# A decoder trunk on one core: squares of a norm summed by two additions of whole chunks instead of one strided reduction

## The chip, the cores and the metric

The kernel runs on one core of one Trainium2 chip. The core has five engines that run their own queues and wait for each other by semaphores: TensorE (PE; its weight loads are listed as PEld), VectorE (DVE), ScalarE (ACT), GpSimd (POOL) and SyncE (SP). The metric is the time of one execution on the device in microseconds (us), as the median of several runs.

## The reference, cut to what matters

Two layers of a decoder trunk are computed for 1040 prompt tokens (16 of them learned) and 32 sample tokens, with a model width of 1024. Each layer has a mixer and an MLP, and each of these four is preceded by an RMS norm over the 1024 features:

```
def rmsnorm(x, g):
    xf = x.astype(jnp.float32)
    y = xf * lax.rsqrt(jnp.mean(xf * xf, axis=-1, keepdims=True) + EPS)
    return (y * g.astype(jnp.float32)).astype(x.dtype)
...
for layer in range(DEPTH):
    h = rmsnorm(x, norm_mix[layer])
    ...
    x = x + sqrelu_mlp(rmsnorm(x, norm_mlp[layer]), w_up[layer], w_down[layer])
```

What is left out is the mixer, a projection with convolution and attention in layer 0 and a pooling mixer in layer 1. The change lies in the sum of squares inside the mean of this norm.

## The kernel before

The residual stream `xT` stays in SBUF as 128 partitions x 8 chunks x 1072 tokens: a token's 1024 features lie in 128 partitions of 8 chunks. The tokens are worked on in three pieces of 368, 352 and 352 columns. All large products are done in fp32 by three matmuls each: activations and weights are split into a high and a low part (`act_hi`, `act_lo`, `w_hi`, `w_lo`), and `product` (L525 to L527) sums three of the four cross products. PE works through units of output, each in one of four PSUM banks; before a unit it waits until the bank's old content has been taken away (`out_freed`), which DVE mostly does.

A norm n (0 to 3) of piece p goes through these steps:

- ACT writes `act_hi` (the residual times the gain, L1052) and DVE `act_lo` (L1394).
- ACT squares four chunks (half 0, then half 1) into `norm_buf` (L1028, `norm_square`). There is one buffer, so the square of half 1 waits until half 0 has been summed (`norm_summed`).
- DVE sums the four chunks of the buffer into one row of columns of `norm_sum` (L1371, `norm_reduce`). This is the place of the change. It runs 24 times: 4 norms x 3 pieces x 2 halves.
- PE adds over the partitions with a matmul against a constant matrix (L581, `norm_stats`; L576 for norm 2), ACT takes the root (L1043), DVE the reciprocal (L1386, `norm_rsqrt`).

The order on each engine is written out by hand, program by program, and is the same before and after apart from the sums. In the first stage (norm 0, about the first 120 us) the steps of a norm are interleaved with the first 18 units of the input projection. ACT copies token tiles from PSUM to the residual (L1075, after PE has transposed them, L605). For a unit that holds queries or keys DVE multiplies by the norm's reciprocal root in PSUM (L1455), ACT squares it (L1124), PE averages it per head (L591), ACT takes the root (L1109), and `head_finish` on DVE takes the reciprocal (L1427) and writes the scaled product, `k_flat` or `qT` (L1433), which frees the bank. So in DVE's queue the two sums of a piece stand ahead of the L1455, L1427 and L1433 that free a bank for PE.

In the pooling stage (about 1210 to 1285 us) DVE scales products of PE into `z` (L1734) and adds windowed means to the residual (L1747, `add_windows`); the sums of norm 3 stand between those.

Two lines tie ACT and PE to the sums, the first in `norm_square`, before it overwrites the buffer, the second in `norm_stats`, which needs both halves:

```
act.wait_ge(norm_summed, i)
...
pe.wait_ge(norm_summed, 2 * k + 2)
```

Of the kernel before, what the change touches and what calls it, by code (L numbers as in the profile page):

```python
# [1 line left out]

# [7 lines left out]
ALU = mybir.AluOpType  # L33
ACT = mybir.ActivationFunctionType
AX_X = mybir.AxisListType.X
# [118 lines left out]
def trunk_kernel(nc, ins, outs):  # L154
# [5 lines left out]
    with ctx:  # L160
        def sem(name):
            return ctx.enter_context(nc.semaphore(name))
# [128 lines left out]

        norm_sq, norm_summed, norm_mean = sem("norm_sq"), sem("norm_summed"), sem("norm_mean")
        norm_root, norm_rs_done = sem("norm_root"), sem("norm_rs_done")
        norm_hi = sem("norm_hi")
        act_ready = sem("act_ready")
        head_scaled = sem("head_scaled")
        head_sq_done, head_mean = sem("head_sq_done"), sem("head_mean")
# [24 lines left out]
        def norm_pieces(n):  # L322
            return PIECES if n < 3 else PIECES1

        def norm_tensors(n):
            return (norm_buf0, norm_sum0) if n == 0 else (norm_buf, norm_sum)
# [1020 lines left out]
        def _(dve):  # L1347
# [16 lines left out]
            def norm_reduce(n, p, half_):  # L1364
                i = 2 * (3 * n + p) + half_
                c0, c1 = norm_pieces(n)[p]
                buf, total = norm_tensors(n)
                dve.wait_ge(norm_sq, i + 1)
                if i >= 2:
                    dve.wait_ge(norm_mean, i // 2)  # L1370
                nc.vector.tensor_reduce(total[:, half_, 0:c1 - c0], buf[:, :, 0:c1 - c0].rearrange("p c n -> p n c"),  # L1371
                                        AX_X, ALU.add).then_inc(norm_summed, 1)

            def norm_rsqrt(n, p):
                k = 3 * n + p
# [23 lines left out]
            def norm_splits(n, p):  # L1399
                for pair in range(4):  # L1400
                    norm_split_lo(n, p, pair)
                for half_ in range(2):
                    norm_reduce(n, p, half_)
# [6 lines left out]
            for pair in range(4):  # L1410
                norm_split_lo(0, 0, pair)
            norm_reduce(0, 0, 0)
            split_lo(1)
            norm_reduce(0, 0, 1)
            norm_rsqrt(0, 0)
            split_lo(2)
# [29 lines left out]
            for m in range(18):  # L1446
                grp, p, part = m // 9, (m % 9) // 3, m % 3
                c0, c1 = PIECES[p]
                n = c1 - c0
# [374 lines left out]
```

## Time and profile before

| | us |
|---|---|
| median of 3 runs (2044.83 to 2045.99) | 2045.95 |
| span of the profiled execution | 2043.0 |
| median less that span | 2.95 |
| PE busy | 2004.9 (98%) |
| DVE busy | 967.2 (47%) |
| ACT busy | 539.9 (26%) |
| POOL busy | 45.5 (2%) |

The span runs from the first to the last instruction of one profiled execution; the execution's own time beside it is not listed, and the median of the runs lies 2.95 us above the span. Busy times are sums over an engine's instructions. Times inside the profile count from the span's start.

### The profile page before, as it was taken

The page shows a single profiled execution, that of the slowest core. Times are in us where ns is not written, and L with a number is a line of the kernel's source. Part 1 is how long each engine was busy: PE and PEld are TensorE (multiplying, and loading weights), DVE is VectorE, ACT ScalarE, POOL GpSimd, SP SyncE. Part 2 cuts the span into 40 slices and gives each one's busy share as a digit, 9 for nine tenths or more (in the row PEclk, how much of TensorE's full clock was granted, in tenths as well). Part 3 has the DMA queues.
Part 4 walks back from the last instruction along what each step waited for, and adds up shares of the span by engine and source line. Part 5 has one row for each costly group of instructions (what it writes and reads, how often), then busy time and mean ns, then how long its engine had stood idle before and what let it go on. Part 6 is the DMA issues. An engine that isn't in the chain of part 4 may idle for free.

```text
span 2043.0 us, 30495 instructions
## 1 busy us (share of the span) xinstructions
PE 2004.9 (98%) x12458; PEld 1959.0 (96%) x12458; DVE 967.2 (47%) x1604; ACT 539.9 (26%) x965; POOL 45.5 (2%) x88
## 2 busy tenths in 40 slices
PE   6999999999999999999999999999999999999999
PEld 5888888999999999999999999999999999999998
DVE  5777776484333333333333487633333333333433
ACT  5333333143122121213121333313121221212131
POOL 1210000100000000000000000000000000000000
PEclk8899999999999999999999998999999999999999
DMA  5411101312111120211211110111211111211112
GB/s 204 146 47 32 32 32 58 99 42 61 42 42 41 41 62 21 62 41 41 62 41 42 42 42 5 31 53 41 62 41 41 41 41 41 62 31 51 52 32 85
DMA packets 132336, 106.42 MB, mean 52 GB/s; under 512 B 4771, under 2 KB 126919, under 8 KB 132240
## 3 DMA queue, kind: packets, MB, share of 16 engines
q1 hardware_dynamic: 126800, 90.52, 14.7%
q0 software_dynamic: 5216, 14.78, 2.3%
q8 instruction: 53, 0.87, 0.2%
q14 instruction: 19, 0.16, 0.0%
q10 hardware_dynamic: 248, 0.09, 0.0%
HBM read 94.64 MB, written 10.49 MB: 51 GB/s over the span
## 4 chain that ended last, share of the span: by engine, by line
PE 91%; DVE 6%; ACT 2%; issue 1%; DMA 0%; SPq 0%; DVEq 0%; ACTq 0%
PE out L525 29%; PE out L527 28%; PE out L526 28%; PE out L950 2%; PE turned L744 1%; DVE norm_sum L1371 1%; DVE head_sq L1427 1%; PE turned L727 1%; DVE act_lo L1394 1%; PE scores L693 1%; PE turned L581 0%; DVE w_lo L1361 0%; DMA raw<-in_w_in_even 0%; DVE rs L1386 0%; ACT act_hi L1052 0%
## 5 line engine op out<-in xcount | busy, mean ns | idle before, releaser
L525 PE MATMUL out<-act_hi,w_hi 128*128 128x352 f32 (+1 forms) x2160 | 714.9, 331 | 6.5 <-DVE qT L1433 2.8
L527 PE MATMUL out<-act_hi,w_lo 128*128 128x352 f32 (+1 forms) x2160 | 703.1, 326 | 0.0
L526 PE MATMUL out<-act_lo,w_hi 128*128 128x352 f32 (+1 forms) x2160 | 700.9, 325 | 0.0
L525 PE MATMUL out<-hid_hi,w_hi 128*128 128x352 f32 (+1 forms) x1536 | 501.3, 326 | 0.0
L527 PE MATMUL out<-hid_hi,w_lo 128*128 128x352 f32 (+1 forms) x1536 | 499.6, 325 | 0.0
L526 PE MATMUL out<-hid_lo,w_hi 128*128 128x352 f32 (+1 forms) x1536 | 497.7, 324 | 0.0
L525 PEld LDWEIGHTS out<-act_hi,w_hi 128*128 128x128 f32 x2160 | 408.3, 189 | 19.3 <-issue 12.3
L526 PEld LDWEIGHTS out<-act_lo,w_hi 128*128 128x128 f32 x2160 | 409.0, 189 | 1.4 <-issue 0.2
L527 PEld LDWEIGHTS out<-act_hi,w_lo 128*128 128x128 f32 x2160 | 408.2, 189 | 0.0
L1636 DVE TENSOR_TENSOR residual<-out,residual 128x352 f32<-128x352 f32 (+1 forms) x408 | 213.1, 526 | 399.2 <-PE out L527 398.8
L1011 ACT ACTIVATE w_hi<-raw 128x1024 fp32r<-128x1024 f32 x156 | 161.2, 1052 | 633.6 <-PE out L527 632.9
L525 PEld LDWEIGHTS out<-hid_hi,w_hi 128*128 128x128 f32 x1536 | 289.1, 188 | 0.0
L526 PEld LDWEIGHTS out<-hid_lo,w_hi 128*128 128x128 f32 x1536 | 288.6, 188 | 0.0
L527 PEld LDWEIGHTS out<-hid_hi,w_lo 128*128 128x128 f32 x1536 | 287.9, 187 | 0.0
L1249 ACT ACTIVATE sq<-relu 128x352 f32<-128x352 f32 (+1 forms) x192 | 96.0, 500 | 509.6 <-DVE relu L1671 509.6
L1671 DVE SCALAR_TENSOR_TENSOR relu<-out,rs 128x352 f32<-128x352 f32 (+1 forms) x192 | 101.1, 527 | 261.2 <-PE out L527 261.0
L1361 DVE TENSOR_TENSOR w_lo<-raw,w_hi 128x1024 fp32r<-128x1024 f32 x156 | 188.3, 1223 | 70.9 <-ACT w_hi L1011 70.8
L1677 DVE TENSOR_TENSOR hid_lo<-sq,hid_hi 128x352 fp32r<-128x352 f32 (+1 forms) x192 | 101.4, 528 | 212.0 <-ACT hid_hi L1251 212.0
L1251 ACT ACTIVATE hid_hi<-sq 128x352 fp32r<-128x352 f32 (+1 forms) x192 | 96.1, 500 | 6.1
L1052 ACT ACTIVATE act_hi<-residual,prm 128x352 fp32r<-128x352 f32 (+1 forms) x96 | 49.4, 583 | 76.8 <-DVE residual L1636 54.3
L1371 DVE TENSOR_REDUCE norm_sum<-norm_buf 128x352 f32<-128x1408 f32 (+1 forms) x24 | 64.6, 2692 | 6.2 <-ACT norm_buf L1028 6.2
L1394 DVE SCALAR_TENSOR_TENSOR act_lo<-residual,prm,act_hi 128x352 fp32r<-128x352 f32 (+1 forms) x96 | 50.1, 586 | 7.1 <-ACT act_hi L1052 7.0
(172 smaller groups left out, 928.4 us busy)
## 6 DMA issues: line engine op xcount, KB each, us to landing
raw<-in_w_up SPq DMA_DIRECT2D x64, 512.0 KB, 4.2
raw<-in_w_down SPq DMA_DIRECT2D x64, 512.0 KB, 3.5
raw<-in_w_in_even SPq DMA_DIRECT2D x18, 512.0 KB, 3.9
raw<-in_w_out_even SPq DMA_DIRECT2D x8, 512.0 KB, 3.5
out_y_prompt<-y_rows SPq DMA_DIRECT2D x8, 512.0 KB, 2.7
x_rows<-in_x_prompt SPq DMA_DIRECT2D x7, 512.0 KB, 7.5
x_spill<-residual POOLq DMA_DIRECT2D x2, 1408.0 KB, 6.1
x_again<-x_spill POOLq DMA_DIRECT2D x16, 176.0 KB, 2.6
```

Source lines behind the costliest of these rows:

```text
L525: nc.tensor.matmul(out, lhs[0], rhs[0], start=first, stop=False)
L526: nc.tensor.matmul(out, lhs[0], rhs[1], start=False, stop=False)
L527: return nc.tensor.matmul(out, lhs[1], rhs[0], start=False, stop=last)
L1011: nc.scalar.activation(w_hi[:, w % 4, :], raw[:, w % 2, :], ACT.Copy).then_inc(w_hi_done, 1)
L1249: nc.scalar.activation(sq[:, q % 2, 0:n], relu[:, q % 2, 0:n], ACT.Square).then_inc(hid_sq_done, 1)
L1251: nc.scalar.activation(hid_hi[p][:, chunk, 0:n], sq[:, q % 2, 0:n], ACT.Copy)\
L1361: nc.vector.tensor_tensor(w_lo[:, w % 4, :], raw[:, w % 2, :], f32(w_hi[:, w % 4, :]), ALU.subtract)\
L1371: nc.vector.tensor_reduce(total[:, half_, 0:c1 - c0], buf[:, :, 0:c1 - c0].rearrange("p c n -> p n c"), AX_X, ALU.add).then_inc(norm_summe ...
L1394: ins_ = nc.vector.scalar_tensor_tensor(out=act_lo[:, c, c0:c1], in0=xT[:, c, c0:c1], scalar=gain(n, c), in1=f32(act_hi[:, c, c0:c1]), op0 ...
L1636: nc.vector.tensor_tensor(xT[:, oc, c0:c1], out_bank[m % 4][:, 0:c1 - c0], xT[:, oc, c0:c1], ALU.add)\
L1671: nc.vector.scalar_tensor_tensor(out=relu[:, q % 2, 0:n], in0=out_bank[m % 4][:, 0:n], scalar=0.0, in1=rs[:, c0:c1], op0=ALU.max, op1=ALU. ...
L1677: nc.vector.tensor_tensor(hid_lo[p][:, chunk, 0:n], sq[:, q % 2, 0:n], f32(hid_hi[p][:, chunk, 0:n]), ALU.subtract).then_inc(hid_ready, 1)
```

## The change

The strided reduction of a half, which reads the four chunks of `norm_buf` column by column, becomes two additions. The first adds chunks 2 and 3 to chunks 0 and 1, in place in `norm_buf`. The second adds chunk 1 to chunk 0 and writes `norm_sum`. A new semaphore, `norm_paired`, makes the second wait for the first. The order of the four summands differs from that of the reduction; nothing else does.

```
-        norm_hi = sem("norm_hi")
+        norm_hi, norm_paired = sem("norm_hi"), sem("norm_paired")
...
                 dve.wait_ge(norm_sq, i + 1)
                 if i >= 2:
                     dve.wait_ge(norm_mean, i // 2)
-                nc.vector.tensor_reduce(total[:, half_, 0:c1 - c0], buf[:, :, 0:c1 - c0].rearrange("p c n -> p n c"),
-                                        AX_X, ALU.add).then_inc(norm_summed, 1)
+                first, second = buf[:, 0:2, 0:c1 - c0], buf[:, 2:4, 0:c1 - c0]
+                nc.vector.tensor_tensor(first, first, second, ALU.add).then_inc(norm_paired, 1)
+                dve.wait_ge(norm_paired, i + 1)
+                nc.vector.tensor_tensor(total[:, half_, 0:c1 - c0], buf[:, 0, 0:c1 - c0], buf[:, 1, 0:c1 - c0], ALU.add)\
+                    .then_inc(norm_summed, 1)
```

The line numbers of the changed kernel are smaller, by 23 ahead of the sums and by 20 behind them, since blank lines at its top are gone: L1371 becomes L1349 and L1351.

This is DVE's queue in the first norm, piece 1, before (`norm_buf_86` and `norm_sum_89` are the buffers of that norm):

```order
L1394 SCALAR_TENSOR_TENSOR act_lo<-residual,prm,act_hi 128x352
L1371 TENSOR_REDUCE norm_sum_89<-norm_buf_86 128x352 [waits norm_mean,norm_sq] x2
L1455 TENSOR_TENSOR out<-out,rs 128x368 [waits out_ready]
L1427 RECIPROCAL head_sq<-head_sq 128x368 [waits head_root,head_scaled]
L1433 SCALAR_TENSOR_TENSOR k_flat<-out,prm,head_sq 128x368 [waits head_rs_done]
L1386 RECIPROCAL rs<-rs 128x352 [waits norm_root]
```

And the same place on DVE in the changed kernel:

```order
L1374 SCALAR_TENSOR_TENSOR act_lo<-residual,prm,act_hi 128x352
L1349 TENSOR_TENSOR norm_buf_86<-norm_buf_86 128x2x352 [waits norm_mean,norm_sq]
L1351 TENSOR_TENSOR norm_sum_89<-norm_buf_86 128x352 [waits norm_paired]
L1349 TENSOR_TENSOR norm_buf_86<-norm_buf_86 128x2x352 [waits norm_mean,norm_sq]
L1351 TENSOR_TENSOR norm_sum_89<-norm_buf_86 128x352 [waits norm_paired]
L1435 TENSOR_TENSOR out<-out,rs 128x368 [waits out_ready]
L1407 RECIPROCAL head_sq<-head_sq 128x368 [waits head_root,head_scaled]
L1413 SCALAR_TENSOR_TENSOR k_flat<-out,prm,head_sq 128x368 [waits head_rs_done]
```

Each reduction has become a pair at the same place, and the instructions behind keep their order.

This is DVE's queue in the pooling stage, norm 3, piece 0, before:

```order
L1734 TENSOR_SCALAR z<-out,rs_rows 96x512 [waits out_ready] x2
L1371 TENSOR_REDUCE norm_sum<-norm_buf 128x352 [waits norm_mean,norm_sq]
L1747 SCALAR_TENSOR_TENSOR residual<-out,prm,residual 128x128 [waits out_ready]
L1747 SCALAR_TENSOR_TENSOR residual<-out,prm,residual 128x128 x3
L1747 SCALAR_TENSOR_TENSOR residual<-out,prm,residual 128x128 [waits out_ready]
L1747 SCALAR_TENSOR_TENSOR residual<-out,prm,residual 128x128 x3
L1371 TENSOR_REDUCE norm_sum<-norm_buf 128x352 [waits norm_mean,norm_sq]
L1734 TENSOR_SCALAR z<-out,rs_rows 128x512 [waits out_ready] x2
```

And in the changed kernel:

```order
L1714 TENSOR_SCALAR z<-out,rs_rows 96x512 [waits out_ready] x2
L1349 TENSOR_TENSOR norm_buf<-norm_buf 128x2x352 [waits norm_mean,norm_sq]
L1351 TENSOR_TENSOR norm_sum<-norm_buf 128x352 [waits norm_paired]
L1727 SCALAR_TENSOR_TENSOR residual<-out,prm,residual 128x128 [waits out_ready]
L1727 SCALAR_TENSOR_TENSOR residual<-out,prm,residual 128x128 x3
L1727 SCALAR_TENSOR_TENSOR residual<-out,prm,residual 128x128 [waits out_ready]
L1727 SCALAR_TENSOR_TENSOR residual<-out,prm,residual 128x128 x3
L1349 TENSOR_TENSOR norm_buf<-norm_buf 128x2x352 [waits norm_mean,norm_sq]
L1351 TENSOR_TENSOR norm_sum<-norm_buf 128x352 [waits norm_paired]
L1714 TENSOR_SCALAR z<-out,rs_rows 128x512 [waits out_ready] x2
```

Here, too, a pair stands where a reduction stood.

## Rows read from the trace of the kernel before

**Rows 1.** The page: PE's busy time, and the granted clock in 40 slices.

```profile
PE 2004.9 (98%) x12458; PEld 1959.0 (96%) x12458; DVE 967.2 (47%) x1604; ACT 539.9 (26%) x965; POOL 45.5 (2%) x88
...
PEclk8899999999999999999999998999999999999999
```

**Rows 2.** PE's waits: total us, times, longest us.

```profile
PE turned L581 <- DVE norm_sum L1371: 6.5, 3, 2.9
...
PE out L525 <- DVE k_flat L1433: 2.2, 2, 1.4
```

**Rows 3.** Groups of DVE instructions by form: busy us, mean ns, idle before.

```profile
L1677 DVE TENSOR_TENSOR hid_lo<-sq,hid_hi 128x352 fp32r<-128x352 f32 x160 | 84.0, 525 | 176.0 <-ACT hid_hi L1251 176.0
...
L1371 DVE TENSOR_REDUCE norm_sum<-norm_buf 128x352 f32<-128x1408 f32 x18 | 47.8, 2654 | 5.8 <-ACT norm_buf L1028 5.8
...
L1512 DVE TENSOR_REDUCE soft<-scores_sb 128x4 f32<-128x1024 f32 x14 | 17.1, 1220 | 0.5
...
L1597 DVE TENSOR_TENSOR act_lo<-qT,act_hi 128x1408 fp32r<-128x1408 f32 x2 | 3.2, 1620 | 0.0
```

**Rows 4.** Timeline, first 25 us: start, us, instruction [idle before <-releaser].

```profile
17.98 2.82 DVE L1371 TENSOR_REDUCE norm_sum<-norm_buf 128x368 f32<-128x1472 f32 x1
...
20.89 1.43 ACT L1028 ACTIVATE norm_buf<-residual 128x1472 f32<-128x1472 f32 x1 [2.00 <-DVE norm_sum L1371]
...
22.95 1.06 PE L605 MATMUL scores<-const,x_rows 128*128 128x128 f32 x8 [1.63 <-ACT residual L1075]
```

**Rows 5.** DVE's timeline, first norm, pieces 1 and 2.

```profile
40.39 2.74 DVE L1371 TENSOR_REDUCE norm_sum<-norm_buf 128x352 f32<-128x1408 f32 x1 [0.98 <-ACT norm_buf L1028]
44.63 2.54 DVE L1371 TENSOR_REDUCE norm_sum<-norm_buf 128x352 f32<-128x1408 f32 x1 [1.51 <-ACT norm_buf L1028]
...
63.16 2.67 DVE L1371 TENSOR_REDUCE norm_sum<-norm_buf 128x352 f32<-128x1408 f32 x1
67.35 2.53 DVE L1371 TENSOR_REDUCE norm_sum<-norm_buf 128x352 f32<-128x1408 f32 x1 [1.51 <-ACT norm_buf L1028]
...
70.35 2.35 DVE L1427 RECIPROCAL head_sq<-head_sq 128x352 f32<-128x352 f32 x1
72.74 0.58 DVE L1433 SCALAR_TENSOR_TENSOR k_flat<-out,prm,head_sq 128x352 f32<-128x352 f32 x1
```

**Rows 6.** PE's timeline, 47 to 82 us.

```profile
47.22 2.71 PE L581 MATMUL turned<-norm_sum,const 128*128 128x352 f32 x4 [2.85 <-DVE norm_sum L1371]
50.80 0.66 PE L525 MATMUL out<-act_hi,w_hi 128*128 128x352 f32 x1 [0.87 <-DVE k_flat L1433]
...
69.93 2.09 PE L581 MATMUL turned<-norm_sum,const 128*128 128x352 f32 x4 [2.52 <-DVE norm_sum L1371]
73.38 0.66 PE L525 MATMUL out<-act_hi,w_hi 128*128 128x352 f32 x1 [1.35 <-DVE k_flat L1433]
...
74.43 0.49 PE L525 MATMUL out<-act_hi,w_hi 128*128 128x352 f32 x1
...
77.07 0.49 PE L525 MATMUL out<-act_hi,w_hi 128*128 128x352 f32 x1
...
80.24 0.32 PE L525 MATMUL out<-act_hi,w_hi 128*128 128x352 f32 x1
...
81.68 0.32 PE L525 MATMUL out<-act_hi,w_hi 128*128 128x352 f32 x1
```

**Rows 7.** PE's timeline, second norm, piece 1.

```profile
438.65 1.45 PE L581 MATMUL turned<-norm_sum,const 128*128 128x352 f32 x4 [1.14 <-DVE norm_sum L1371]
```

**Rows 8.** Timelines of DVE and PE in the pooling stage.

```profile
1246.32 2.72 DVE L1371 TENSOR_REDUCE norm_sum<-norm_buf 128x352 f32<-128x1408 f32 x1
...
1250.22 3.72 PE L950 MATMUL out<-band,z 96*128 96x96 f32 x32 [0.96 <-DVE residual L1747]
...
1254.27 0.39 PE L525 MATMUL out<-w_hi,act_hi 128*128 128x256 f32 x1 [0.33 <-DVE z L1734]
```

**Rows 9.** A window: length, busy us (count) of each engine, granted clock, DMA share, GB/s.

```profile
31.60:34.00 2.40, 0.04 (x1) 0.08 (x2) 1.21 (x2) 1.16 (x3) 0.00 (x0) 1.00 0.23 67
```

## The prediction

> **What bounds the kernel now.** The busy shares come first: TensorE (PE) is busy for 2004.9 of the 2043.0 us of the span [rows 1]. Nearly all the time is matmul work that the change does not touch. VectorE (DVE) work, such as the squares that are summed, can give time back only where PE stands still and a DVE instruction ends that wait. So the second view is PE's own list of waits [rows 2]. It puts 6.5 us in three waits down to the strided sum itself (L1371) and 2.2 us in two waits down to k_flat (L1433), an instruction that stands behind the sums on DVE's queue. The remaining places are read from timelines of the stretches where those waits lie.
>
> There are 24 strided sums, two for each of four norms and three pieces. All 24 become shorter, but with no PE wait near them most will only give DVE more idle time. The question is therefore the price of one sum, and which of the 24 PE waits for.
>
> **Price of one sum.** The 18 sums of 4 chunks x 352 columns take 2654 ns on average [rows 3]. What replaces one is an addition over 2 x 352 = 704 columns and one over 352. Two rows of the same kind of instruction with all operands in SBUF give the line: 352 columns take 525 ns, and 1408 columns (4 x 352, a view in several pieces like the new one) take 1620 ns [rows 3]. That is 1095 ns for 1056 columns, 1.037 ns each, plus 160 ns. So 704 columns cost 160 + 730 = 890 ns, and the pair 890 + 525 = 1415 ns. The second addition waits for the first. Such a pair on DVE, a reciprocal followed by the product that reads it, shows 70.35 + 2.35 = 72.70 and then a start at 72.74: 0.04 us [rows 5]. A sum therefore costs 1.455 us. At 368 columns the same line gives 160 + 763 + 160 + 382 + 40 = 1.505 us, against 2.82 us for the first sum of the kernel [rows 4]. Each sum saves about 1.2 to 1.3 us, some 29 us of DVE's busy time over 24 sums.
>
> A rule speaks against this. The contiguous reduction over 1024 elements takes 1220 ns, 1.19 ns an element, while the strided one takes 2654 / 1408 = 1.88 [rows 3]. The Trainium skill, page "VectorE: DVE Perf Modes", section "The perf-mode tier table", gives tensor_reduce and fp32 tensor_tensor the same one-element rate; by that alone a sum of 1408 elements would cost about what an addition of 1408 does, 1.62 us by the row, and the change would save 0.17 us a sum. The trace here disagrees with it for the strided form, by its 2654 ns. I take the row. The rule gives the rival "only an equal rate" below.
>
> **Place 1: the first norm, piece 0.** The sum of half 0 starts at 17.98 and takes 2.82 us. ScalarE (ACT) may square half 1 into the same buffer only after it, at 20.89, having idled 2.00 us for it. Behind that square on ACT's queue stand the copies of the next token tiles, and PE idles 1.63 us until the first copy, at 22.95 [rows 4]. With 1.505 us the square starts 1.31 us earlier. The wait of 1.63 leaves 0.32, so nothing else takes over: **-1.31**. The rest of the stage (norm statistics, root, reciprocal, product, next copies) hangs on this chain and moves with it.
>
> **Place 2: first norm, piece 1.** The two sums take 2.74 (from 40.39) and 2.54 us (from 44.63), with the square of half 1 between them and no slack [rows 5]. PE waits 2.85 us for the second one at 47.22, computes statistics, and waits 0.87 us more for k_flat, until 50.80 [rows 6]. k_flat follows the sums on DVE through a product and a reciprocal. Both sums count: 2.74 + 2.54 - 2 x 1.455 = **-2.37** at k_flat and hence at PE's next unit. The earlier wait nearly vanishes, but what is late next is k_flat, so the gain is what DVE saves, not the 2.85 us of the wait. In between, DVE and ACT hand the work to each other (reciprocal, product, square, the splits of piece 2) down to the sums of piece 2, so the shift is carried there.
>
> **Place 3: first norm, piece 2.** The same picture: sums of 2.67 (63.16) and 2.53 us (67.35), PE waits 2.52 at 69.93 and 1.35 for k_flat at 73.38 [rows 5, 6]. 2.67 + 2.53 - 2 x 1.455 = **-2.29**.
>
> **Place 4: second norm, piece 1.** PE waits 1.14 us for a sum at 438.65 [rows 7]. That sum and the one before it on DVE save 2.4 us together, so the wait ends: **-1.14**. It can give no more.
>
> **Place 5: the pooling stage.** The sum at 1246.32 (2.72 us) delays the residual products behind it, and PE waits 0.96 us for them at 1250.22. The next sum delays the scalings behind it, and PE waits 0.33 us for them at 1254.27 [rows 8]. Both savings exceed the waits: **-1.29**.
>
> The other sums lie beside matmuls without a PE wait. Their cover is PE's queue of units; they are worth nothing here, and their cost is nothing in either kernel. The added semaphore step is in the 0.04 us.
>
> Sum: 1.31 + 2.37 + 2.29 + 1.14 + 1.29 = **8.40 us**.
>
> **The clock.** After the waits of places 2 and 3 the matmuls run at half clock (1.2 instead of 2.4 GHz): between 74.43 and 77.07 nine of them start 0.293 us apart, between 80.24 and 81.68 nine start 0.160 apart [rows 6]. After place 2 this is covered by DVE. After place 3 it is not: from 73.38 to about 77.4 some 14 matmuls lose 0.133 us each, 1.8 us. A standstill of 2.37 us, between 31.60 and 33.95, left the granted clock at 1.00 [rows 9]. In the changed kernel the standstill ahead of PE's restart is split and shorter: PE's unit would end near 63.7 (67.41 - 3.68, the gains of places 1 and 2), the statistics start near 63.9 and last some 1.4 us (1.45 at full clock [rows 7]), and k_flat would come at 73.32 - 5.97 = 67.35, so PE idles about 2.0 us at a stretch. That lies below the 2.37 that did no harm and not far from the 2.52 that did. I count half of the 1.8: **-0.9**. Sum with it: 9.3 us.
>
> **Rivals.**
> - *Something else is late next.* If only places 2 and 3 arrive in full, because copies, statistics or other DVE work take over elsewhere, 4.7 us come: 2041.3. For it: in the first 80 us PE, ACT and DVE wait for each other in turn, so a shorter link can lay bare another. Against: each chain was followed to the instruction that is late next. Chance 0.13.
> - *Only an equal rate* (the rule above). Seven sums on the path save 0.17 each: 1.2 us, 2044.8, no change that can be told. Against it stand the 2654 ns. Chance 0.04.
> - *Slower: the second addition's wait.* If a dependent addition had to wait long for the first one's write, seven pairs on the path would pay it. It cancels the gain at 2.65 - 1.415 = 1.24 us a pair; at twice that, 2.5 us, the seven pairs lose 8.7 us: 2054.7. Against: 0.04 us in the rows. Chance 0.03, with all else that could slow the kernel.
> - *The clock holds throughout.* All of the 1.8 us after place 3 comes back, and as much again (an estimate: a stretch of the same length) if one of the dips of the granted clock in the pooling stage, the 8 in the second half of the row of the page [rows 1], goes too: 8.4 + 1.8 + 1.8 = 12.0 us, 2034.0. Chance 0.10.
> - *My forecast*, places 1 to 5 with half of the clock's loss: chance 0.70, with a range of its own of 8.0 to 10.5 us (2035.5 to 2038).
>
> **The numbers.** The median of the runs shown is 2045.95, 2.95 us above the span of the profiled execution, and I leave what lies around the span as it is. 2045.95 - 9.3 = **2036.6 us** (a span of about 2033.7). The range goes from the clock's best case, less 0.5 us for the spread of the runs, to the case of places 2 and 3 alone: 2033.5 to 2041.3, and leaves out about 0.15. A measurement tells about 0.2% (4.1 us) from no change, that is anything below 2041.9 is faster. Forecast and clock case (0.80) count as faster, and of the first rival two thirds (0.09): **0.89**. Same: its last third and the equal rate, **0.08**. Slower: **0.03**.
>
> **What would show it.** Additions of about 0.89 and 0.53 us in place of 2.65; DVE busy some 29 us less. ACT's second square at 19.6 instead of 20.89, and PE's turn at 21.6 instead of 22.95. The restarts at 50.80 and 73.38 moved to about 47.1 and 67.4. No wait at PE near 437 - 6 = 431, and none in the pooling stage near 1243. PE's waits for the sums gone from its list, its waits for k_flat longer in their place. Wrong if the additions measure over 1.2 us for 704 columns, if the restarts come later than 48 and 69, or if half clock lasts longer than before after either of them.

## The result, and the profile after

The changed kernel takes 2034.11 us (median of 5 runs, 2029.50 to 2035.45). The kernel before takes 2045.42 us (5 runs, 2044.26 to 2045.99) on the same chip. The ratio of the two sets of runs is 0.9937, with a 95% interval of 0.9925 to 0.9949: faster by 0.63%, 12.9 us of 2045.4 (10.4 to 15.3). The medians alone lie 11.3 us apart, the means 12.7. The forecast was 9.3 us, with a range for the time down to 2033.5; 0.9937 of the 2045.95 us it started from is 2033.1. The direction is right, the gain was put too small.

The profiled execution of the changed kernel took 2029.53 us, the second shortest of the five, with a span of 2027.7 us against 2043.0 before. These two profiles thus lie 15.3 us apart, more than the runs do; what the pair shows beyond the change stands below the table of stretches. What answers to [rows 1] on its page:

```profile
PE 1993.5 (98%) x12458; PEld 1949.7 (96%) x12458; DVE 937.7 (46%) x1628; ACT 540.1 (27%) x965; POOL 45.5 (2%) x88
...
PEclk9999999999999999999999999999999999999999
```

DVE has 24 instructions more and 29.5 us less work. PE is busy for 11.4 us less on the same 12458 matmuls, which are no less work: some of them ran at a higher clock. The row of the granted clock says the same; the digits 8 of before, at the start and in the second half, are gone.

PE's list of waits (total us, times, longest us) answers to [rows 2]:

```profile
PE out L502 <- DVE qT L1413: 5.3, 3, 3.0
PE scores L582 <- ACT residual L1052: 4.2, 3, 2.4
PE out L502 <- DVE k_flat L1413: 3.4, 2, 2.0
...
PE turned L558 <- DVE norm_sum L1351: 0.2, 1, 0.2
```

The 6.5 us of waits for the sums have become 0.2 us. The waits for k_flat have grown from 2.2 to 3.4 us, since PE now reaches them sooner. DVE's groups by form (busy us, mean ns, idle before) answer to [rows 3]:

```profile
L1349 DVE TENSOR_TENSOR norm_buf<-norm_buf 128x704 f32<-128x704 f32 x18 | 15.9, 886 | 5.8 <-ACT norm_buf L1005 5.8
...
L1351 DVE TENSOR_TENSOR norm_sum<-norm_buf 128x352 f32<-128x352 f32 x18 | 9.5, 525 | 0.6
```

The additions take 886 and 525 ns, where 890 and 525 were worked out. The timelines of DVE, ACT and PE (start, us, instruction, idle before it) answer to [rows 4 to 6]:

```profile
18.32 0.93 DVE L1349 TENSOR_TENSOR norm_buf<-norm_buf 128x736 f32<-128x736 f32 x1
...
19.92 1.43 ACT L1005 ACTIVATE norm_buf<-residual 128x1472 f32<-128x1472 f32 x1 [0.68 <-DVE norm_sum L1351]
...
21.98 1.07 PE L582 MATMUL scores<-const,x_rows 128*128 128x128 f32 x8 [1.46 <-ACT residual L1052]
...
39.41 0.89 DVE L1349 TENSOR_TENSOR norm_buf<-norm_buf 128x704 f32<-128x704 f32 x1 [0.97 <-ACT norm_buf L1005]
40.34 0.52 DVE L1351 TENSOR_TENSOR norm_sum<-norm_buf 128x352 f32<-128x352 f32 x1
...
44.75 1.34 PE L558 MATMUL turned<-norm_sum,const 128*128 128x352 f32 x4
47.46 0.43 PE L502 MATMUL out<-act_hi,w_hi 128*128 128x352 f32 x1 [1.36 <-DVE k_flat L1413]
...
59.82 0.88 DVE L1349 TENSOR_TENSOR norm_buf<-norm_buf 128x704 f32<-128x704 f32 x1
...
59.96 0.43 PE L502 MATMUL out<-act_hi,w_hi 128*128 128x352 f32 x1 [3.01 <-DVE qT L1413]
...
64.28 1.45 PE L558 MATMUL turned<-norm_sum,const 128*128 128x352 f32 x4 [0.17 <-DVE norm_sum L1351]
67.73 0.43 PE L502 MATMUL out<-act_hi,w_hi 128*128 128x352 f32 x1 [2.00 <-DVE k_flat L1413]
```

From the first sum of a piece to PE's restart the three chains are 3.66, 8.05 and 7.91 us long. Before, they were 4.97, 10.41 and 10.22 us [rows 4 to 6]. The gains are 1.31, 2.36 and 2.31 us, 5.98 together.

PE's first and last turn of the first stage and the first and last band matmul of the pooling stage cut the span into pieces. These are the rows of the lines (count, shortest, median and longest ns, first to last start) in the kernel before:

```profile
L605 PE MATMUL scores<-const,x_rows x72: 221/273/448, 5.3 to 40.1; 128*128 128x128 f32 x64, 48*128 48x48 f32 x8
...
L629 PE MATMUL scores<-const,cache_rows x8: 272/272/273, 84.2 to 85.0; 128*128 128x128 f32 x8
...
L950 PE MATMUL out<-band,z x288: 182/275/534, 1213.2 to 1280.7; 128*128 128x128 f32 x48, 128*128 128x16 f32 x48, 112*128 112x112 f32 x8, 112*128 112x16 f32 x8
...
L950 PE MATMUL out<-band,z_states x16: 276/401/402, 1270.5 to 1281.2; 120*128 120x32 f32 x16
```

And in the changed kernel:

```profile
L582 PE MATMUL scores<-const,x_rows x72: 221/273/448, 5.9 to 40.7; 128*128 128x128 f32 x64, 48*128 48x48 f32 x8
...
L606 PE MATMUL scores<-const,cache_rows x8: 272/273/273, 78.3 to 79.0; 128*128 128x128 f32 x8
...
L927 PE MATMUL out<-band,z x288: 182/275/454, 1205.9 to 1265.5; 128*128 128x128 f32 x48, 128*128 128x16 f32 x48, 112*128 112x112 f32 x8, 112*128 112x16 f32 x8
...
L927 PE MATMUL out<-band,z_states x16: 276/338/401, 1256.6 to 1266.0; 120*128 120x32 f32 x16
```

| stretch | before | after | difference | chain as forecast |
|---|---|---|---|---|
| start, to the first turn | 5.3 | 5.9 | +0.6 | 0 |
| first stage (places 1 to 3) | 78.9 | 72.4 | -6.5 | -5.97 |
| up to the pooling stage (place 4) | 1129.0 | 1127.6 | -1.4 | -1.14 |
| pooling stage (place 5) | 68.0 | 60.1 | -7.9 | -1.29 |
| rest of the span | 761.8 | 761.7 | -0.1 | 0 |

The first stage lies near its chains. The stretch up to the pooling stage varies by more than its difference: it is 1129.0 to 1130.1 us in three profiles of the kernel before, and 1127.6 and 1130.3 in two of the changed kernel. Place 4 is therefore read from a shorter stretch, with the experiments on norm 1.

The pooling stage gives back six times what its two waits were worth, but in this pair not all of that comes from the change. From 10 to 26 us behind the stage's first band matmul, ahead of both waits and with no wait of PE in it, the granted clock differs between profiles of one and the same program (a window's row: length, busy us and count of PE, PEld, DVE, ACT, POOL, granted clock, DMA share, GB/s). The kernel before, in the profile used so far and in its third one:

```profile
1223.20:1239.20 16.00, 15.92 (x116) 15.85 (x115) 9.48 (x36) 4.10 (x11) 0.00 (x0) 0.79 0.01 2
1224.60:1240.60 16.00, 15.92 (x143) 15.85 (x142) 11.96 (x43) 6.90 (x14) 0.05 (x1) 1.00 0.01 3
```

The changed kernel, in the profile used so far and in its second one:

```profile
1215.90:1231.90 16.00, 16.00 (x145) 15.97 (x143) 10.99 (x35) 6.90 (x14) 0.20 (x1) 1.00 0.01 3
1218.50:1234.50 16.00, 16.00 (x119) 15.97 (x117) 8.50 (x29) 4.18 (x11) 0.00 (x0) 0.79 0.01 2
```

The stage takes 68.0 and 62.4 us in the first two, 60.1 and 64.8 us in the last two. So the -7.9 of the table sets a profile with this early half clock against one without it. The last section of the experiments compares like with like.

### The profile page after: what moved, and what is told of

It reads as the page before. It is cut to its first block, busy times and chain, and to the rows that moved or that the text cites. A ratio compares the mean times of both kernels' runs of the same rounds, so it can differ in the third digit from the quotient of the medians.

```text
span 2027.7 us, 30519 instructions
## 1 busy us (share of the span) xinstructions
PE 1993.5 (98%) x12458; PEld 1949.7 (96%) x12458; DVE 937.7 (46%) x1628; ACT 540.1 (27%) x965; POOL 45.5 (2%) x88
## 4 chain that ended last, share of the span: by engine, by line
PE 93%; DVE 4%; ACT 2%; issue 0%; DMA 0%; SPq 0%; DVEq 0%; ACTq 0%
PE out L502 29%; PE out L504 29%; PE out L503 29%; PE out L927 2%; PE turned L721 1%; DVE head_sq L1407 1%; PE turned L704 1%; PE scores L670 1%; PE turned L558 0%; DVE w_lo L1338 0%; DVE act_lo L1374 0%; DMA raw<-in_w_in_even 0%; DVE conv_y L1559 0%; ACT w_hi L988 0%; ACT scores_sb L1148 0%
## 5 line engine op out<-in xcount | busy, mean ns | idle before, releaser
L1148 ACT ACTIVATE scores_sb<-scores_sb,soft 128x256 f32<-128x256 f32 (+2 forms) x72 | 33.4, 464 | 60.6 <-DVE soft L1495 60.6
```

## The experiments

"Additions in norm n" means the loop of the sums takes the new pair there and the strided reduction elsewhere. The cuts of code below leave out what stays the same and the counter that replaces `i + 1`. Where a mean difference is given, it is between the means of all runs of the kernel and of before in the same series, with about two standard errors.

**Additions in norm 0 alone** (places 1 to 3).

```
+                if n in (0,):
+                    (the two additions)
+                else:
                     nc.vector.tensor_reduce(...)
```

> Additions in the first norm alone, the strided sums stay in the other three. Places 1 to 3 of the chain give 5.97 us, so the restarts of PE come at about 47.1 and 67.4 and the time is about 2039.5. Theory A (the clock in the pooling stage follows from the waits that the sums of that stage cause): the pooling stage keeps its 68 us, and 2039 to 2040 results. Theory B (where half clock falls in the pooling stage is chance, whichever sums run): the stage is now and then 2 to 7 us shorter in single runs, and the times scatter over 2033 to 2040.

Measured: 2036.86 us (7 runs) against 2044.06 (23), ratio 0.9969 (0.9957 to 0.9980), mean difference -6.5 +- 1.5 us. The chains' 5.98 us account for nearly all of it.

**Additions in norm 3 alone** (place 5): `if n in (3,):`.

> Additions in the last norm alone (pooling stage). The chain gives 1.29 us there (PE's waits of 0.96 and 0.33 us vanish). Theory A: the clock in the stage comes back too, 2 to 7 us more, so 2037 to 2042 and a pooling stage of 60 to 65 us. Theory B: 2044.1 on average, with single runs 2 to 7 us lower as in any kernel.

Measured: 2039.54 us (11 runs) against 2044.06, ratio 0.9979 (0.9970 to 0.9988), mean difference -4.1 +- 1.2 us. Two waits of 1.29 us together are three times overpaid. Something beside the chain is gained there.

**Additions in norms 1 and 2 alone** (place 4): `if n in (1, 2):`.

> Additions in the second and third norm alone. The chain gives 1.14 us at place 4 (PE's wait at 438.65 vanishes): 2044.3. Both theories have no more, except that by theory B single runs may be 2 to 7 us lower; if the last sum of the third norm, which lies in the pooling stage, matters for the clock there, 2040 to 2043.

Measured: 2045.53 us (11 runs) against 2044.06, ratio 1.0008 (0.9999 to 1.0017), mean difference +1.3 +- 1.4 us. No gain is seen.

**The changed kernel again,** with no edit.

> The changed kernel once more, for a second profile of it. The chain to the start of the pooling stage should be 7.1 us shorter than before in this profile as well (within 0.5 us), and PE's waits in the pooling stage absent. Theory A: the stage takes 60 to 64 us again. Theory B: it takes anything from 60 to 67 us, with low stretches of the clock at other places than in the first profile.

Measured: 2029.63 us (5 runs, 2028.87 to 2036.96) against 2044.06, ratio 0.9938 (0.9924 to 0.9952), mean difference -12.2 +- 3.3 us. The first result is repeated. Single runs of one kernel scatter by some 8 us.

**Additions in two sums only,** norm 3, piece 0: `if (n, p) == (3, 0):`. These are the two sums ahead of the waits of 0.96 and 0.33 us [rows 8].

> Additions only for the two sums of the last norm's piece 0 (at 1246 and 1251 us), strided sums everywhere else. Theory A (PE's waits of 0.96 and 0.33 us behind these two sums are what costs time in the pooling stage, themselves and a low stretch of the clock near 1255 that follows them): the whole effect of the last norm, about 4.2 us, comes from these two, 2039 to 2041, and the low stretch near 1255 is absent. Rival: the other four sums of that norm, beside them, matter as much: only 1.3 us, 2042.7.

Measured: 2039.76 us (11 runs) against 2044.28 (29), ratio 0.9985 (0.9976 to 0.9994), mean difference -3.8 +- 1.4 us. Two of 24 sums give all that norm 3 gives, as far as the errors tell, and three times their waits. The windows of 10 us from the start of the band matmuls on 96 columns, which stood behind the 0.96 wait, show the clock there. Before:

```profile
1250.20:1260.20 10.00, 9.65 (x64) 9.14 (x64) 7.95 (x17) 1.54 (x4) 0.00 (x0) 0.83 0.01 2
```

With additions in these two sums alone:

```profile
1247.10:1257.10 10.00, 10.00 (x84) 9.57 (x83) 7.19 (x20) 3.54 (x9) 0.00 (x0) 1.00 0.01 2
```

PE does 84 matmuls in place of 64, with a granted clock of 1.00 in place of 0.83.

The kernel before was profiled twice more, with no edit, for this window.

> The kernel before, for a second profile. If the pooling stage's half clock is laid down by the waits of its two sums: a low stretch that begins within some 6 us behind the waits of 0.96 and 0.33 us, as in the first profile, and a stage of 65 to 71 us. If it is chance: a stage near 60 us is seen here too.

> The kernel before, for a third profile, with the same expectations as the second.

Measured: 2050.67 and 2041.10 us, with a granted clock of 0.66 and 0.83 in the window and a pooling stage of 71.1 and 62.4 us (from its first to its last band matmul). The first of them:

```profile
1255.00:1265.00 10.00, 10.00 (x58) 9.89 (x59) 7.35 (x17) 0.42 (x2) 0.00 (x0) 0.66 0.01 2
```

The clock behind the wait falls in each of the three, but not equally long: 58 to 66 matmuls in 10 us, against 84. The stage of 62.4 us lies in neither of the two expected ranges: its half clock behind the wait is there, the early one is not.

**The sums made as long as before.** The additions stay, and a maximum of three chunks with themselves goes ahead of them in all 24 sums. Its values change nothing.

```
-                first, second = buf[:, 0:2, 0:c1 - c0], buf[:, 2:4, 0:c1 - c0]
+                first, second, m = buf[:, 0:2, 0:c1 - c0], buf[:, 2:4, 0:c1 - c0], buf[:, 1:4, 0:c1 - c0 - 30]
+                nc.vector.tensor_tensor(m, m, m, ALU.max).then_inc(norm_paired, 1)
+                dve.wait_ge(norm_paired, 2 * i + 1)
                 nc.vector.tensor_tensor(first, first, second, ALU.add).then_inc(norm_paired, 1)
-                dve.wait_ge(norm_paired, i + 1)
+                dve.wait_ge(norm_paired, 2 * i + 2)
```

> The additions, preceded in every sum by a maximum of three chunks with themselves (30 columns short), about 1.2 us, which changes no value and brings a sum back to about 2.65 to 2.75 us. If the duration of a sum is all that the change acts by: the time of before, 2043 to 2046, PE's waits back at 47, 70, 438 and 1250. Rival (the kind of instruction matters, by what it does to memory or to other engines): 2034 to 2040 in spite of the padding.

Measured: 2044.55 us (12 runs) against 2044.28, ratio 1.0005 (0.9997 to 1.0014), mean difference +0.9 +- 1.3 us. DVE's groups show a sum of 1160 + 893 + 526 ns, 2.58 us:

```profile
L1349 DVE TENSOR_TENSOR norm_buf<-norm_buf 128x966 f32<-128x966 f32 x18 | 20.9, 1160 | 5.8 <-ACT norm_buf L1005 5.8
...
L1351 DVE TENSOR_TENSOR norm_buf<-norm_buf 128x704 f32<-128x704 f32 x18 | 16.1, 893 | 0.6
...
L1353 DVE TENSOR_TENSOR norm_sum<-norm_buf 128x352 f32<-128x352 f32 x18 | 9.5, 526 | 0.6
```

PE's list of waits:

```profile
PE turned L558 <- DVE norm_sum L1353: 6.6, 3, 2.9
...
PE out L927 <- DVE residual L1729: 0.9, 1, 0.9
```

PE's waits for the sums and for what stands behind them are back, and the gain is gone, the clock's part too. So it comes from how long a sum takes; anything else about the additions is worth no more than the error of this difference allows.

**The reduction kept, its stride taken away.** ACT writes the squares so that the four chunks of a column lie side by side, and the reduction reads them in order.

```
+                by_column = buf.rearrange("p c n -> p (c n)")[:, 0:4 * (c1 - c0)].rearrange("p (n c) -> p n c", c=4)
+                nc.vector.tensor_reduce(total[:, half_, 0:c1 - c0], by_column, AX_X, ALU.add)
```

> The reduction stays, but ACT writes the squares with the four chunks of a column side by side, so that the reduction reads without a stride. If the stride cost the time: the reduction takes 1.6 to 1.7 us in place of 2.65, and 8 of 10 parts of the gain come, 2034 to 2038, unless ACT's strided write is slower. If the reduction itself is slow (rival): 2.65 us again and 2044, or worse by ACT.

Measured: 2043.50 us (11 runs) against 2044.28, ratio 0.9999 (0.9990 to 1.0008). The groups by form:

```profile
L1006 ACT ACTIVATE norm_buf<-residual 128x1408 f32<-128x1408 f32 x18 | 49.5, 2750 | 17.2 <-DVE norm_sum L1350 17.2
...
L1350 DVE TENSOR_REDUCE norm_sum<-norm_buf 128x352 f32<-128x1408 f32 x18 | 29.1, 1615 | 16.3 <-ACT norm_buf L1006 16.3
```

And a row of PE's list of waits:

```profile
PE scores L582 <- ACT residual L1053: 6.5, 2, 4.1
```

The reduction falls from 2654 to 1615 ns, to the 1620 ns of an addition of as many elements [rows 3]. The square rises from 1371 ns before to 2750 ns. Square and sum together go from 4.02 to 4.37 us. The stride's cost has moved to ACT, and with it the wait of place 1: PE waits 4.1 us for the first copy now, until 24.59, where it waited 1.63 us, until 22.95 [rows 4].

**A product between the two sums of a piece.** In the changed kernel, the product of units 2 and 5 of the first stage, which stood behind both sums, goes between them, into DVE's wait for the second square.

```
+                if m in (2, 5):
+                    norm_reduce(0, p + 1, 1)
                 if m >= 2:
                     finish(m - 2)
...
                 if m in (1, 4):
-                    for half_ in range(2):
-                        norm_reduce(0, p + 1, half_)
+                    norm_reduce(0, p + 1, 0)
```

> The changed kernel with the product L1435 of units 2 and 5 moved between the two sums of a piece in the first norm, into the 1.5 us in which DVE waits for the square of half 1. If k_flat's chain on DVE is what PE's restart waits for, the product's 0.54 us leave the chain twice: restarts near 46.9 and 66.6, 1.1 us less than the changed kernel. Rival: ACT (its square of half 1, the head's root) is late next: no change.

Measured: 2028.72 us (6 runs, 2026.37 to 2034.23) against 2044.28, ratio 0.9933 (0.9917 to 0.9948), mean difference -14.5 +- 2.7 us. From the first sum of a piece to k_flat DVE's chain is 6.87 us long for piece 1 and 6.75 for piece 2 in its profile, against 7.39 and 7.26 in the changed kernel: shorter by 0.52 and 0.51 us, the product's length, as expected. PE's first stage is 69.8 us long, against 72.4 and 72.8 in two profiles of the changed kernel, but it is 70.9 in both profiles that have the same sums in norm 0 without this move. The time can't be told from that of the changed kernel (0.9937, 0.9938).

**Additions in norms 0 and 3 together:** `if n in (0, 3):`.

> Additions in the first and the last norm, strided sums in the second and third. If the parts add up (6.5 and 4.1 us alone): 2033.5. If the second and third norm are needed for the rest of the gain, as the whole change (12 us) less these parts suggests, it stays at 2033 to 2036; if they cost time here too, as they did alone (1.3 us slower), it is 2030 to 2032 and faster than the whole change.

Measured: 2035.23 us (5 runs) against 2044.35 (23), ratio 0.9953 (0.9938 to 0.9967), mean difference -9.9 +- 1.9 us. The two parts alone add up to 10.6, so they are additive as far as this can tell.

**Additions in norm 1 alone, and in norm 2 alone:** `if n == 1:`, `if n == 2:`.

> Additions in the second norm alone. PE's wait of 1.1 us near 438 vanishes: 2042.9 by the chain. If the loss of 1.3 us with both the second and third norm sits here: 2045 to 2046, with more half clock in the attention's end or behind place 4 than before. Otherwise 2042 to 2043.5.

> Additions in the third norm alone; no wait of PE hangs on them, so 2044.0 by the chain. If the loss sits here, because DVE reaches the work of the pooling stage earlier and PE's half clock there lasts longer: 2045 to 2047. Otherwise 2043.5 to 2044.5.

Measured: 2045.82 us (12 runs) and 2044.82 us (11 runs) against 2044.35, ratios 1.0001 (0.9993 to 1.0010) and 1.0001 (0.9992 to 1.0010). Norm 1 alone was profiled twice more:

> Additions in the second norm alone, for a second profile. The chain is 1.1 to 1.6 us shorter up to the pooling stage. If the time is 2046 and the mean granted clock 0.987, as in 7 of 12 runs, the profile shows where the clock takes it back: in the attention's end (two low stretches near 330 to 350 instead of one or none), in the first 80 us, or in the pooling stage (over 68 us).

> Additions in the second norm alone, for a third profile, with the same expectations as the second.

Measured: 2043.98 and 2044.74 us, beside 2042.82 for before on the same chip. Norm 2 gives nothing, as was expected. In the profiles with additions in norm 1 the stretch between two matmuls on either side of place 4, the statistics of norm 1 for piece 0 and for piece 2, is 1.4 us shorter: 41.15 to 41.16 us in seven profiles, against 42.46 to 42.63 in ten without. Before:

```profile
420.74 1.40 PE L581 MATMUL turned<-norm_sum,const 128*128 128x368 f32 x4
...
463.31 1.35 PE L581 MATMUL turned<-norm_sum,const 128*128 128x352 f32 x4
```

And in the changed kernel:

```profile
414.93 1.40 PE L558 MATMUL turned<-norm_sum,const 128*128 128x368 f32 x4
...
456.08 1.35 PE L558 MATMUL turned<-norm_sum,const 128*128 128x352 f32 x4
```

The time doesn't show it.

**The pooling stage over all profiles.** Its length, taken as in the table above, by what sums norm 3, piece 0, has, and by whether the clock was below 1.00 early, from 10 to 26 us behind the stage's first band matmul:

| sums there | early half clock | profiles | length, us | clock in the 10 us from the 96-column block |
|---|---|---|---|---|
| as long as before | yes | 7 | 65.4 to 71.1, mean 68.4 | below 1.00 in 7 |
| as long as before | no | 3 | 62.4 to 65.5, mean 64.4 | below 1.00 in 3 |
| additions | yes | 2 | 64.5 and 64.8, mean 64.65 | below 1.00 in 0 |
| additions | no | 4 | 59.7 to 60.7, mean 60.2 | below 1.00 in 1 |

With the additions the stage is 4.2 us shorter among the profiles without early half clock and 3.7 among those with it, or 2.7 if two of the seven are left out, whose early clock is 0.68 where the others have 0.79. Over all ten and all six the means are 67.2 and 61.7 us, 5.5 apart, but that also counts the early half clock, which is worth some 4 us and fell in 7 of 10 profiles against 2 of 6. The rows as long as before hold the padded kernel as well. The kernel without the stride is in neither: it keeps the wait of 0.3 us, has a clock of 0.83 there, and its stage is 61.2 us long. The first stage has a mean of 79.3 us in 11 profiles with the strided sums in norm 0 (78.2 to 80.2), and of 71.8 us with the additions in 4 (70.9 to 72.8).

## Why the prediction fell short

**Price of one sum: right.** 886 + 525 ns and a step of some 0.04 us. The padded kernel shows that this duration is the cause. The *equal rate* rival is out for the strided form. The unstrided form bears out its rule: the Trainium skill, page "VectorE: DVE Perf Modes", section "The perf-mode tier table", puts reduction and addition at the same one-element rate, and 1615 against 1620 ns agree with it. What the strided reduction pays, 2654 - 1615 = 1039 ns, is the price of its stride.

**Places 1 to 3: right,** at 1.31, 2.36 and 2.31 us against 1.31, 2.37 and 2.29. What is late next is what was named: the next token tiles, then k_flat. The statistics start without a wait (44.75) or with 0.17 us (64.28). One thing was not seen ahead: at 59.96 PE now waits 3.01 us for qT, since the units ahead run at full clock and finish sooner (in the second profile of the changed kernel, with a granted clock of 0.86 in the window from 44 to 56, the wait is 1.78 us). It costs nothing, since DVE's chain to the sum at 59.82 sets the pace.

**Place 4: as forecast in the profile, not shown in the time.** The stretch around it is 1.4 us shorter, 1.14 forecast. Norm 1 alone gives no gain in its runs; its interval reaches down to 0.9993, which is 1.4 us. Whether the time loses these 1.4 us again elsewhere, or the scatter hides them, stays open.

**Place 5: the waits as forecast, their worth not.** Both waits are gone from PE's list, 1.29 us. The sum of the chains is 1.31 + 2.36 + 2.31 + 1.4 + 1.29 = 8.7 us, where 8.40 was forecast.

**The clock: the step that failed.** The term for the clock was counted at 0.9 us, half of one loss after place 3, and place 5 at its two waits alone, with nothing for the clock behind them. The runs show about 1.5 us in the first stage and about 2.5 in the pooling stage. The result less the chains leaves 12.9 - 8.7 = 4.2 us (1.7 to 6.6). In the first stage the mean lengths differ by 7.5 us, 1.5 more than the chains, so that part was too small by about 0.6. The windows behind places 2 and 3 show where it comes from. Before:

```profile
46.00:58.00 12.00, 9.91 (x31) 8.24 (x31) 10.96 (x13) 5.87 (x14) 8.74 (x16) 0.57 0.48 156
69.00:81.00 12.00, 9.71 (x38) 8.23 (x39) 9.25 (x9) 3.47 (x6) 0.00 (x0) 0.72 0.05 15
```

And after:

```profile
44.00:56.00 12.00, 10.64 (x60) 9.40 (x58) 10.95 (x15) 7.21 (x16) 8.74 (x16) 1.00 0.72 243
63.00:75.00 12.00, 9.83 (x45) 8.55 (x45) 9.49 (x10) 3.57 (x7) 0.00 (x0) 0.86 0.08 23
```

Behind place 2 the clock holds in this profile, and the 3.01 us of waiting for qT take up what that gives. Behind place 3 it still falls, for a shorter time: the idle stretch of 2.00 us was worked out exactly. But the ground for counting half does not hold. The clock fell behind 2.00 us, less than the 2.37 that "did no harm", and in the changed kernel half clock follows the standstill of [rows 9] itself, which is 2.38 us there (a row of PE's timeline and a window behind it):

```profile
32.98 1.06 PE L582 MATMUL scores<-const,x_rows 128*128 128x128 f32 x8 [2.38 <-ACT residual L1052]
...
34.00:38.00 4.00, 4.00 (x17) 4.00 (x16) 3.62 (x8) 4.00 (x10) 0.00 (x0) 0.57 0.10 31
```

Before, the window from 34 to 38 us has a granted clock of 1.00. The length of a standstill does not tell whether half clock follows.

The larger part lies in the pooling stage. There the wait of 0.96 us (about 1 us in each) went with a clock of 0.66 to 0.83 in the 10 us behind it, in every one of ten profiles; with the wait gone it fell in one of six. The second wait of 0.33 us is missing in four of the ten, where the 96-column matmuls already ran slower. That stage's half clock stood in the row of the page [rows 1] and was only weighed in the rival *the clock holds throughout*, which gives 2034.0 us and is nearest to the result, with a chance of 0.10; its number is near, but the clock did not hold throughout. The additions in these two sums alone give 3.8 +- 1.4 us, 2.5 more than the waits. The stage lengths, like with like, put it at 1.4 (2.7 - 1.29) to 2.9 us (4.2 - 1.29). With the 1.5 of the first stage that makes 2.9 to 4.4 in all, beside the 4.2 that the result leaves. It rests on few profiles and is known to some 2 us, no closer, since half clock does not fall in the same places in every run. Whether the additions also change how often the early half clock of the pooling stage comes stays open.

*Something else is late next* and *the second addition's wait* did not come about: all five places arrived, and the step between the additions is 0.04 us.

## What to carry to other kernels

Price a reduction by whether its inner axis is contiguous. Then find the few instances that the bound engine waits for; here some 7 of 24 sums carry the chain's gain, and two of them most of the clock's. Where a wait of the bound engine is followed by work at half clock, its removal can give more than its own length (here 3.8 us for waits of 1.29), and the time of those matmuls at either level belongs in the sum. Before the lengths of one stage are compared between two profiles, see whether half clock that comes and goes between runs of one program lies in either. A stride is not gained by handing it to the engine that writes: compare the sum of both instructions.

## What the hardware showed that was not expected

- On DVE, a reduction of 1408 fp32 elements takes 2654 ns when neighbouring summands lie a chunk apart, and 1615 ns when they lie side by side: 1.88 against 1.15 ns an element.
- On ACT, the square of 1408 elements takes 1371 ns when it writes in order, and 2750 ns when each element lands four places from the last.
- A standstill of PE of about 1 us in the pooling stage went with half clock behind it in ten of ten profiles. A standstill of 3.01 us ahead of 59.96 is followed by a granted clock of 1.00 in the changed kernel's profile:

```profile
59.96:65.00 5.04, 4.87 (x27) 4.37 (x28) 3.43 (x6) 2.12 (x3) 0.00 (x0) 1.00 0.46 160
```

In three other profiles with additions in norm 0 the same standstill, 3.02 to 3.03 us long, is followed by half clock (0.50 to 0.72 from 59 to 65 us). A wait's length alone doesn't tell what follows.

- Half clock also came with no standstill near it: from 10 to 26 us into the pooling stage PE was busy for 15.91 to 16.00 of 16 us, and the granted clock was 0.79 or 0.68 in 9 of 17 profiles and 1.00 in the others, in profiles of one program as well.
- Runs of the kernel before range from 2040.47 to 2050.67 us over all series, and two of its profiles have pooling stages of 62.4 and 71.1 us.
